# Layer boundaries: the low parts of the weights of keys (first half) and values are formed by GpSimd in place of VectorE

## The reference, cut to what matters

```python
def second_block(x, meta_tokens, ln_in_g, ln_in_b, w_in, ...):
    h = jnp.concatenate([meta, x], axis=1)
    h = _layer_norm(h, ln_in_g, ln_in_b)          # boundary 1
    for l in range(DEPTH_2):                      # 2 layers
        h = _hybrid_layer(h, pos, w_in[l], ...)
    return h[:, N_META:]

def _hybrid_layer(h, pos, w_in, ...):
    proj = h @ w_in                               # 528 x 2048 @ 2048 x 5120
    (c_val, c_glu, c_gate, q, k, v, a_gate, r_x, r_gate) = jnp.split(proj, split_pts, axis=-1)
    ...
    mixed = jnp.concatenate([y_conv, y_attn, y_lru], axis=-1) @ w_out
    return _layer_norm(DEEPNORM_ALPHA * h + mixed, ln_post_g, ln_post_b)   # boundary 2 after layer 0
```

## Time and profile before

| | |
|---|---|
| median of 3 runs | 3387.51 us (3386.51 to 3388.33) |
| profiled execution, its own time | 3386.99 us |
| its span, first to last instruction | 3385.4 us |
| TensorE matmul busy | 3289.8 us, 97% of the span |
| VectorE busy | 1742.2 us, 51% |
| ScalarE busy | 1369.0 us, 40% |
| GpSimd busy | 323.9 us, 10% |
| mean granted clock of TensorE | 0.986 of full speed |

### The profile page before, as it was taken

One profiled execution on the slowest core, in us unless ns is written; L12 is line 12 of the kernel. 1 busy time (PEld: TensorE's weight loads), 2 busy tenths in 40 slices (PEclk: granted clock), 3 DMA queues, 4 the chain that ended last, 5 costly groups with the idle time before them and its releaser, 6 DMA issues.

```text
span 3385.4 us, 53971 instructions
## 1 busy us (share of the span) xinstructions
PE 3289.8 (97%) x19734; PEld 2899.4 (86%) x19734; DVE 1742.2 (51%) x2525; ACT 1369.0 (40%) x2173; POOL 323.9 (10%) x323
## 2 busy tenths in 40 slices
PE   8999999999999999899979999999997999999997
PEld 7889888888888888788878999999997988888786
DVE  6332333435444444424686555556558565556647
ACT  5332323334333333323235454555325455545424
POOL 1000000000000000000000412432000133313000
PEclk9999999999999999999989999999998999999998
DMA  6322322333333232422324222221433422221422
GB/s 197 99 87 86 99 87 87 93 94 97 89 97 89 86 100 79 140 88 93 99 93 150 69 77 76 75 71 53 161 99 109 136 76 74 70 80 60 154 88 86
DMA packets 367157, 325.41 MB, mean 96 GB/s; under 512 B 23768, under 2 KB 362648, under 8 KB 365360
## 3 DMA queue, kind: packets, MB, share of 16 engines
q1 hardware_dynamic: 352064, 290.00, 28.1%
q0 software_dynamic: 5424, 16.44, 1.5%
q10 hardware_dynamic: 9552, 17.37, 1.5%
HBM read 306.66 MB, written 17.07 MB: 96 GB/s over the span
## 4 chain that ended last, share of the span: by engine, by line
PE 52%; DVE 4%; ACT 2%; DVEq 1%; issue 1%; ACTq 0%
PE ps L557 15%; PE ps L558 14%; PE ps L559 14%; PE ps L885 2%; PE ps L926 1%; DVE w_low L1559 1%; DVE residual L1808 1%; PE ps L563 1%; PE ps L564 1%; PE ps L565 1%; PE ps L872 0%; PE ps L900 0%; PE ps L957 0%; PE ps L933 0%; PE ps L904 0%
## 5 line engine op out<-in xcount | busy, mean ns | idle before, releaser
L557 PE MATMUL ps<-x_high,w_high 128*128 128x512 f32 (+3 forms) x4736 | 1640.4, 346 | 57.0 <-DVE w_low L1559 22.3
L558 PE MATMUL ps<-x_low,w_high 128*128 128x512 f32 (+3 forms) x4736 | 1606.2, 339 | 0.0
L559 PE MATMUL ps<-x_high,w_low 128*128 128x512 f32 (+3 forms) x4736 | 1600.5, 338 | 0.0
L1559 DVE TENSOR_TENSOR w_low<-w_raw,w_high 128x1024 fp32r<-128x1024 f32 x540 | 657.0, 1227 | 1001.8 <-ACT w_high L1053 977.1
L557 PEld LDWEIGHTS ps<-x_high,w_high 128*128 128x128 f32 x4736 | 896.8, 189 | 170.5 <-issue 66.3
L558 PEld LDWEIGHTS ps<-x_low,w_high 128*128 128x128 f32 x4736 | 896.5, 189 | 106.2 <-issue 7.2
L559 PEld LDWEIGHTS ps<-x_high,w_low 128*128 128x128 f32 x4736 | 895.7, 189 | 98.5
L1053 ACT ACTIVATE w_high<-w_raw 128x1024 fp32r<-128x1024 f32 x540 | 569.8, 1058 | 699.5 <-PE ps L559 571.3
L563 PE MATMUL ps<-w_high,x_high 128*128 128x256 f32 x1184 | 332.3, 281 | 3.5 <-DVE w_low L1559 2.7
L564 PE MATMUL ps<-w_high,x_low 128*128 128x256 f32 x1184 | 332.6, 281 | 0.0
L565 PE MATMUL ps<-w_low,x_high 128*128 128x256 f32 x1184 | 332.6, 281 | 0.0
(11 more groups left out here) (367 smaller groups left out, 2520.0 us busy)
## 6 DMA issues: line engine op xcount, KB each, us to landing
w_raw<-in_w_in SPq DMA_DIRECT2D x784, 256.0 KB, 3.1
w_raw<-in_w_out SPq DMA_DIRECT2D x280, 256.0 KB, 2.9
residual<-residual_stream ACTq DMA_DIRECT2D x8, 1056.0 KB, 11.2
residual_stream<-y_layer ACTq DMA_DIRECT2D x2, 2176.0 KB, 10.5
x_natural<-in_x SPq DMA_DIRECT2D x4, 1024.0 KB, 9.1
x_feature_major<-x_stage POOLq DMA_DIRECT2D x4, 1024.0 KB, 6.8
gate_bc<-gate_rows POOLq DMA_DIRECT2D x8, 512.0 KB, 4.4
acc<-x_feature_major POOLq DMA_DIRECT2D x1, 4096.0 KB, 13.4
```

The costliest lines, as they stand in the source:

```text
L557: pe.matmul(dst, wh[:, j, kt, wc], xh[:, k, tok], start=first, stop=False)
L558: pe.matmul(dst, wh[:, j, kt, wc], xl[:, k, tok], start=False, stop=False)
L559: return pe.matmul(dst, wl[:, j, kt, wc], xh[:, k, tok], start=False, stop=last)
L1559: dve.tensor_tensor(wl[:, j], raw[:, j], f(wh[:, j]), ALU.subtract).then_inc(lo_ready, 1)
```

## The change

VectorE's helper calls for the eight low parts of a boundary are taken out. GpSimd gets a function `boundary_lows(l)` that forms them, K's four and then V's four, each once its high part is there and once the piece before it is counted in `lo_ready`. It runs behind the loading of the layer's parameters, ahead of GpSimd's waits for the layer. VectorE waits for the eight pieces before it forms K2's, since `lo_ready` is a common count.

```diff
+            def boundary_lows(l):
+                for U in (U_LAYER + N_LAYER * l + O_K, U_LAYER + N_LAYER * l + O_V):
+                    for j in range(4):
+                        pool.wait_ge(lo_ready, 4 * U + j)
+                        pool.wait_ge(hi_ready, 4 * U + j + 1)
+                        pool.tensor_tensor(wl[:, j], raw[:, j], f(wh[:, j]), ALU.subtract).then_inc(lo_ready, 1)
...
             parameters(0)
+            boundary_lows(0)
...
                     parameters(l + 1)
+                    boundary_lows(l + 1)
...
-                    if d in (6, 7, 8, 9) and K is not None:
-                        low(K, d - 6)
...
                 norm_spread(n, 1)
-                if K is not None:
-                    low(K + 1, 0)
-                    low(K + 1, 1)
                 dve.drain()
                 for d in range(AHEAD):
                     center(n, 1, d)
                 norm_scale(n, 1)
-                if K is not None:
-                    low(K + 1, 2)
-                    low(K + 1, 3)
                 norm_tiles(n, 1, K is not None, lambda d: None)
...
                 dve.memset(small[:, 59:60], LN_EPS)
                 dve.drain()
+                dve.wait_ge(lo_ready, 4 * (U + O_K2))
                 lows(U + O_K2)
```

## The result

The changed kernel takes 3395.82 us in the median of 11 runs (3394.66 to 3398.51), the kernel before 3387.51 us: a ratio of 1.0026 [1.0017, 1.0034], 8.3 us slower. The profiled execution has a span of 3393.6 us against 3385.4. The forecast was 3395.7 us.

A forecast was written before the change was run, and what follows sets the result against it. VectorE's chain up to x_low tile 15 was taken to set the stage's time. K 3.8 + V 0.3 = 4.1 us a boundary, 8.2 for two, on 3386.99, plus 0.5 for the median: 3395.7 us, range 3389.5 to 3401.5.

The forecast's parts named there:

- GpSimd's length: At the boundaries, each low part formed on GpSimd takes 2.2 us, range 1.9 to 2.5.
- The hold: At the boundaries, each GpSimd low part stops VectorE for its length less 0.1 us: 2.1 us.
- K: First half of the tokens: four holds, 8.4 us, less 4.6 us freed, make x_low tile 15 3.8 us later.
- V: Second half of the tokens at each boundary: holds mostly hidden, +0.3 us, with 0 to 0.6 as the ends.
- The sum: Both boundaries: 3.8 + 0.3 = 4.1 us each, 8.2 us together, giving a median of 3395.7 us.
- what comes after the boundaries is TensorE without a wait: Behind the boundaries: TensorE runs without a wait, so the loss of 8.2 us stays.
- The marks: Signs expected in the profile after: GpSimd's sixteen low parts, lengthened VectorE instructions in K's half, TensorE's first wait about 3.5 us shorter.
- Hidden work: Rival at the boundaries: GpSimd doesn't stop VectorE, 4.9 us gained at each, 3377.7 us; chance 0.12.
- Half hidden: Rival: one hold or so per half falls in VectorE's idle time or the reciprocal; 1.5 us a boundary, 3390.5 us; chance 0.15.
- V is late too: Rival in V: reciprocal behind the fourth hold, last piece of pass 1 waits 2.2 us a boundary, 3400.1 us; chance 0.13.

The follow-up runs named there:

- e3: Kernel before plus eight GpSimd subtractions of 128x512 a boundary, reading SBUF beside VectorE's work for K, output unused; 3400.16 us, ratio 1.0039.
- e1: Changed kernel with only K's four low parts a boundary on GpSimd, V's formed by VectorE again; 3395.76 us, ratio 1.0022 to the kernel before.
- e4: Kernel before plus sixteen GpSimd memsets of 128x512 a boundary, four behind each high part of K, writing only; 3386.97 us, ratio 1.0001.
- e6: Changed kernel with each GpSimd low part cut into four instructions of 256 columns; 3402.10 us, ratio 1.0043 to the kernel before.
- e7: Kernel before with K's four low parts on VectorE one tile earlier, the first ahead of tile 4's add; 3388.27 us, ratio 1.0003.

## Why the prediction was right, step by step

- **GpSimd's length.** Taken 2.2 us, range 1.9 to 2.5. The first of a boundary takes 2.34, the others 2.40 to 2.61, mean 2.47: at the upper end. Scaling by columns gave the size; the longest, 2.60 and 2.61, are three that started while an instruction of VectorE was under way.
- **The hold.** Taken 2.1 us, as length less 0.1. Measured 1.98 to 2.15 at the first boundary, as a longer length less 0.3 to 0.5. The two errors cancel. e3 measured the second by itself: 0.7 us lost to 1.04.
- **K.** +3.8 us at tile 15 forecast, +3.66 and +3.88 measured; e1 has the same alone (+8.3 us in time, 7.5 in its trace). All four holds fell ahead of tile 7 as said, and no low part of K is waited for.
- **V.** +0.3 us forecast (0 to 0.6), 0.87 and 0.99 measured. This is the term that was mis-sized. The sum let GpSimd's parts follow each other by 2.4 us; they came every 2.52 (10.09 over four), so the fourth, which starts V's piece 3, is 0.4 us later, counted from K's piece 3. And TensorE, which needs 1.4 us for a piece, now stops for three of them: 0.2 us ahead of piece 1, 0.83 ahead of pieces 2 and 3, where it stopped once for 1.34. Behind each stop the first matmul takes 0.39 us in place of 0.28, and the next starts 0.22 us behind it in place of 0.12. From the starts of its matmuls, the stops and these restarts cost 2.49 us after and 1.61 before: the whole of the 0.87. Of the second boundary's 0.99, 0.14 lie ahead of V, in K's last products. That the reciprocal runs beside a hold was an estimate, which no row of before shows; beside the fourth part it took 1.74 us. The first scaled tile came at 1807.82, as forecast (1803.5 + 3.8, and 0.5 by which the trace's boundary is later).
- **The sum.** 4.1 us a boundary forecast, 4.53 and 4.87 in the traces. That is 9.4 us; the first boundary is reached 0.5 us later as well, and yet the span is only 8.2 longer. The step "what comes after the boundaries is TensorE without a wait" is where the rest sits: between the boundaries the kernel before takes 742.2 us and the kernel after 740.6. The last section tells of it. So the total of 8.3 against 8.2 is partly luck: V 1.3 us too small for both boundaries, this 1.6 not in the sum at all. The forecast's own range was written wider than its terms give: holds of 1.8 to 2.4 us and V of 0 to 0.6, twice, make 3392.7 to 3398.7, not 3392.5 to 3399.5. Nothing hangs on it, since 3395.82 lies inside both.
- **The marks.** Sixteen instructions of 2.3 to 2.6 us on GpSimd, four single instructions of 2.4 to 2.6 us on VectorE a boundary, TensorE's first wait shorter by 3.5 us (12.44 to 8.96), no wait for a low part in K: all as said. The mark "later waits for x_low together about 7 us longer" came out at 6.8 us (10.95, 5.31 and 0.23, against 2.70, 6.8 and 0.24).
- **The rivals.** *Hidden work* (3377.7) is excluded by VectorE's 2.4 to 2.6 us instructions and by e3. *Half hidden* (3390.5) needed holds in idle time; none fell there. *V is late too* (3400.1) needed the reciprocal to fall behind the fourth hold; it ran beside the fourth part (1805.95, in a part that lasts from 1805.8 to 1808.3), and the last x_low of the second half isn't waited for.

## What to carry to other kernels

Work given to an idle GpSimd wasn't free while VectorE read two tensors from SBUF: here each instruction of GpSimd that read SBUF cost VectorE its length less 0.2 to 0.6 us (2.34 to 2.61 us long in the kernel after, 1.04 in e3), so a 1.15 us operation moved became a 2.1 us hold, and cutting it in four made the whole worse, by the time that GpSimd itself then lost. Move to GpSimd only what is done while VectorE isn't on the path, or work that only writes (e4's sixteen memsets a boundary: ratio 1.0001, VectorE's two-input instructions at 0.42 us). And before shortening the longest wait of a stage, ask which instruction its end hangs on: here 4.5 us less of the longest wait gave nothing, while moving some 4 us of work a boundary behind tile 15 gave 4.2 us for the two, and 8.1 with TensorE kept at work in two of its waits (granted clock 1.00 from 1788 to 1803 in place of 0.88).

## What the runs showed of the hardware

**The clock after a short pause.** Between the boundaries, in the first layer, the kernel before has this in the timeline of TensorE and in the stretches of 10 us:

```profile
2103.10 0.36 PE L557 MATMUL ps<-x_high,w_high 128*128 128x264 f32 x1 [1.77 <-issue]
```

```profile
2100.00:2110.00 10.00, 8.23 (x49) 7.79 (x49) 5.45 (x6) 4.91 (x15) 0.00 (x0) 0.83 0.68 211
```

and the kernel after, where the pause ends at 2108.06:

```profile
2108.06 0.36 PE L567 MATMUL ps<-x_high,w_high 128*128 128x264 f32 x1 [1.49 <-issue]
...
2105.00:2115.00 10.00, 8.51 (x64) 8.07 (x64) 7.01 (x8) 5.15 (x16) 0.00 (x0) 1.00 0.69 209
```

The granted clock of 0.83 is a mean: from 2104 to 2107 it is 0.50, and from 2103.93 to 2107.2 the matmuls of 264 columns start every 0.22 us in place of 0.12. That begins 0.8 us behind the end of a pause of 1.77 us. The kernel after keeps 1.00 behind its pause of 1.49 us. Of the ten traces four have the dip (before, e1, e6, e7; pauses of 1.77, 1.77, 1.79 and 1.97 us) and take 742.2 to 742.4 us between the boundaries; the others, with pauses of 1.49 to 1.89 us, don't have it and take 740.6 to 741.1. The length of the pause alone doesn't decide it, and what does isn't settled: the change doesn't touch this work, and one trace of each kernel can't say whether the dip belongs to the kernel or to the execution. It is large enough, 1.6 us, to blur every sum of single microseconds here.

**One instruction longer beside a write.** In e4 one instruction was longer beside a memset, the only one with a tensor and a scalar that meets one: 0.68 us at 1763.64, where its like take 0.35. It reads one tensor only. In e3 the same instruction meets a read and takes 0.95. Beside the memset 0.3 us are lost; the two-input ones around it keep their 0.41 to 0.43 us. It is a single row in one trace, and the time shows nothing of it.
